# All first expert products ahead of the second ones, gates multiplied into an arena of ones, loops unrolled

## What is computed

```python
qh = (xt @ w_query).reshape(T, PEER_HEADS, PEER_KEY_DIM)
s1 = jnp.einsum('thd,nd->thn', qh[..., :half], sub_keys_1)
...
v1, i1 = lax.top_k(s1, PEER_TOPK)
...
top_s, top_j = lax.top_k(cand, PEER_TOPK)
...
u = expert_u[ec]
a = jax.nn.gelu(jnp.einsum('cd,ced->ce', xc, u).astype(jnp.float32), approximate=False)
return jnp.einsum('ce,ced->cd', (gc * a).astype(x.dtype), expert_v[ec])
```

## Time and profile before

| | us |
|---|---|
| time, median of 3 runs | 1217.26 |
| the three runs | 1221.36, 1217.26, 1208.93 |
| profiled execution, span from first to last instruction | 1207.1 |
| PE busy in it | 1091.6 (90%) |
| DVE busy in it | 685.5 (57%) |

### The profile page before, as it was taken

How to read it: one execution, slowest core, us unless ns; L and a number is a source line. 1 busy time by engine, 2 the same in 40 slices (tenths; PEclk the granted TensorE clock), 3 DMA queues, 4 the chain that set the end, 5 groups by cost and what they waited for, 6 DMA issues and landing times.

```text
span 1207.1 us, 19681 instructions
## 1 busy us (share of the span) xinstructions
PE 1091.6 (90%) x6268; PEld 942.4 (78%) x6268; DVE 685.5 (57%) x1678; ACT 480.8 (40%) x800; POOL 249.6 (21%) x332
## 2 busy tenths in 40 slices
PE   6997788979888677779999999999999999999994
PEld 2476667658788666668799999999999999999993
DVE  0112636037799669987755555555555555555554
ACT  0112424111333269963443444444434444444442
POOL 1000000000188858850011111111111111111110
PEclk9995556789988789999999999999999999999997
DMA  9830000050043200036545554555555545545541
GB/s 357 348 140 35 1 0 1 1 209 1 1 140 123 86 36 0 0 118 193 189 172 183 180 202 174 187 195 176 195 186 176 203 177 185 197 174 193 190 156 70
DMA packets 43516, 167.36 MB, mean 139 GB/s; under 512 B 4560, under 2 KB 5600, under 8 KB 41824
## 3 DMA queue, kind: packets, MB, share of 16 engines
q1 hardware_dynamic: 42944, 164.38, 38.0%
q0 software_dynamic: 544, 2.63, 0.5%
HBM read 165.94 MB, written 1.05 MB: 138 GB/s over the span
## 4 chain that ended last, share of the span: by engine, by line
PE 57%; issue 31%; POOL 5%; DVE 4%; ACT 2%; DVEq 1%; DMA 1%; POOLq 0%; ACTq 0%
PE ps L436 57%; POOL lo L403 4%; DVE slab L1296 2%; ACT arena L908 1%; DVE slab L1295 1%; DMA arena<-in_ln 1%; DVE arena L1285 0%; DVEq L1296 0%; DVE xs L1196 0%; DVE xs L1199 0%; DVE xs L1181 0%; PE ps L688 0%; DVE xs L1186 0%; POOL slab L417 0%; ACT L840 0%
## 5 line engine op out<-in xcount | busy, mean ns | idle before, releaser
L436 PE MATMUL ps<-x1hl,hi 128*128 128x256 f32 x2048 | 381.6, 287 | 22.2 <-POOL lo L403 21.4
L436 PEld LDWEIGHTS ps<-x1hl,hi 128*128 128x128 f32 x2048 | 333.2, 196 | 31.6 <-POOL lo L403 13.5
L436 PE MATMUL ps<-hi,ahl 128*128 128x512 f32 x1024 | 294.5, 393 | 3.4 <-DVE lo L1317 3.4
L436 PE MATMUL ps<-x1hl,lo 128*128 128x256 f32 x1024 | 293.5, 287 | 0.0
L1317 DVE TENSOR_TENSOR lo<-slab,hi 128x1024 fp32r<-128x1024 f32 x128 | 156.9, 1226 | 169.5 <-ACT hi L934 169.4
L934 ACT CAST hi<-slab 128x1024 fp32r<-128x1024 f32 x128 | 134.4, 1051 | 278.6 <-PE ps L436 278.6
L436 PEld LDWEIGHTS ps<-hi,ahl 128*128 128x128 f32 x1024 | 185.9, 189 | 37.5 <-issue 3.5
L436 PEld LDWEIGHTS ps<-x1hl,lo 128*128 128x128 f32 x1024 | 200.3, 196 | 0.0
L395 POOL TENSOR_TENSOR gel<-gel,arena 128x256 f32<-128x256 f32 x104 | 76.4, 735 | 577.6 <-ACT gel L940 577.6
L436 PE MATMUL ps<-lo,ahl 128*128 128x512 f32 x512 | 159.1, 392 | 0.0
L436 PE MATMUL ps<-arena 128*128 128x256 f32 (+6 forms) x608 | 153.6, 442 | 5.7 <-DVE arena L1065 2.0
(11 more groups left out here) (162 smaller groups left out, 762.4 us busy)
## 6 DMA issues: line engine op xcount, KB each, us to landing
slab<-in_uT SPq DMA_DIRECT2D x128, 512.0 KB, 4.1
slab<-in_pv SPq DMA_DIRECT2D x128, 512.0 KB, 3.5
arena<-in_w_tok SPq DMA_DIRECT2D x2, 2048.0 KB, 19.9
arena<-in_w_out SPq DMA_DIRECT2D x1, 4096.0 KB, 31.4
arena<-in_wqa SPq DMA_DIRECT2D x1, 4096.0 KB, 12.9
arena<-in_wqb SPq DMA_DIRECT2D x1, 4096.0 KB, 12.2
arena<-in_w_tok SPq DMA_DIRECT2D x4, 512.0 KB, 11.5
arena<-in_w_tok SPq DMA_DIRECT2D x1, 1792.0 KB, 19.3
```

What stands on the lines that cost most here:

```text
L436: return nc.tensor.matmul(o, lhsT, rhs, start=start, stop=stop, skip_group_check=True)
```

## The change

All 128 first products stand ahead of the 128 second ones. During routing DVE makes the rests itself, one by one between its own steps (`fill`, 35 of them), and the three passes over 6400 elements are cut in four pieces. The products of blocks 0 to 39 (`N0`) write their gelus into `arena`; POOL fills the rest of `arena` with 1.0 in two pieces. From block 40 on PE does one group of gates and one first product in turn; DVE multiplies every plate (128 blocks by 4 tokens) into `arena` (`gate_group`) and, one block at a time, the gelus of later blocks (`block_gate`). POOL no longer subtracts or multiplies; it makes two one-hots a group. The second products follow, with eight buffers for v and four for its high part. The transfer of the second norm's weights now starts after eight second blocks are split. Every loop is written out.

```diff
-NPRE = 24
+N0 = 40
+NROUTE = 35
+NTURN = 36
+UR, UH = 6, 3
+VR, VH = 8, 4
...
+            for c in range(NK):
+                if c >= UR:
+                    sp.wait_ge(pe_h, c - UR + 1)
+                sp.dma_start(u_raw(c), uT[c]).then_inc(u_in[c % UR], 16)
+            for c in range(NK):
+                if c == 0:
+                    sp.wait_ge(pe_g, GN)
...
+            pool.wait_ge(q_saved, 2 * PH)
+            nc.gpsimd.memset(arena[:, N0 * S:A_XT], 1.0).then_inc(ones_low, 1)
...
+            pool.wait_ge(rT_saved, T)
+            onehots(0)
+            onehots(1)
+            nc.gpsimd.memset(arena[:, A_XT:A_ALL], 1.0).then_inc(ones_high, 1)
+            for g in range(2, GN):
+                onehots(g)
+
+            pool.wait_ge(a_lo, KD)
             pool.dma_start(ln2_sb, ln2.partition_broadcast(P)).then_inc(l_ln2, 16)
...
+            for c in range(NK):
+                if c == NTURN:
+                    turn_routes()
+                if 0 <= c - N0 < GN:
+                    gates(c - N0)
+                expert_in(c)
...
+            for c in range(NK):
+                expert_out(c)
...
+            for c in range(NK):
+                gelu(c)
+                if c + UH < NK:
+                    u_split(c + UH)
+                if c + UH == NROUTE - 1:
+                    route_exp()
+                if c == NTURN - 1:
+                    save_routes()
+                    act.wait_ge(rT_saved, T)
+                    onehot(0)
+                if 0 <= c - (N0 - 1) < GN - 1:
+                    onehot(c - (N0 - 1) + 1)
...
+            def fill(n=1):
+                for _ in range(n):
+                    c = filled[0]
+                    dve.wait_ge(u_hi, c + 1)
+                    v.tensor_tensor(u_rest_of(c), u_raw(c), hi[:, c % UH, :].bitcast(F32), ALU.subtract).then_inc(u_lo, 1)
+                    filled[0] += 1
...
+            def gate_group(g, blocks):
+                dve.wait_ge(pe_g, g + 1)
+                if g == 0:
+                    dve.wait_ge(ones_low, 1)
+                    dve.wait_ge(ones_high, 1)
+                    dve.wait_ge(gelu_done, N0)
+                if blocks:
+                    dve.wait_ge(gated, blocks)
+                a = G[:, :, 4 * g:4 * g + 4]
+                v.tensor_tensor(a, ps[:, gate_bank(g), :].rearrange("p (q c) -> p c q", q=4), a, ALU.mult
                                 ).then_inc(pre_gated, 1)
...
+            while filled[0] < N0 - 1:
+                fill()
             dve.wait_ge(rT_saved, T)
-            onehots(0, True)
...
+            onehots(0)
+            fill()
+            for g in range(GN):
+                fill()
+                if g + 1 < GN:
+                    onehots(g + 1)
+                gate_group(g, max(0, g - 2))
+                if g >= 2:
+                    block_gate(N0 + g - 2, g + 1)
```

More of the change, by code:

```diff
@@ L337, in _ @@
             sp.wait_ge(pe_memp, 6)
[L339 to L375, removed]
+            for c in range(NK):
[5 more added lines that the diff above has]
+                    sp.wait_ge(pe_g, GN)
+                elif 4 <= c < VR:
+                    sp.wait_ge(pe_h, NK)
+                elif c >= VR:
+                    sp.wait_ge(pe_y, c - VR + 1)
+                sp.dma_start(raw[:, v_slot(c), :], pv[c]).then_inc(v_in[c % VR], 16)
             for t in range(T):
@@ L408, in onehots @@
[L408 to L418, removed]
@@ L667, in products @@
                     for m, (w, part) in enumerate(ws):
-                        last = mm(ps[:, b % 2, 0:S], w, x1hl[:, k, part, :], k == 0 and m == 0,
+                        last = mm(ps[:, c % 2, 0:S], w, x1hl[:, k, part, :], k == 0 and m == 0,
                                   k == KD - 1 and m == 2)
[L670 to L677, removed]
@@ L679, in _ @@
-            pe.wait_ge(x1_split, 2)
[L680 to L713, removed]
-            def expert_out(i, b, first, final):
-                pe.wait_ge(v_lo, i * RB + (b + 1))
-                pe.wait_ge(a_lo, i * RB + (b + 1))
+                last.then_inc(pe_h, 1)
@@ L720, in expert_out @@
[L720 removed]
+                    for m, (part, v) in enumerate(((0, vh), (0, vl), (1, vh))):
                         for half in range(2):
[L722 to L723 removed]
+                            last = mm(ps[:, 4 + 2 * t + half, :], ahl[:, c % 2, part, t * P:(t + 1) * P],
+                                      v[:, half * 512:(half + 1) * 512], c == 0 and m == 0, c == NK - 1 and m == 2)
@@ L952, in _, with gelu @@
-            with act.Fori(1, NM) as j:
-                for b in range(RB):
-                    u_split(j, b, False)
-                    gelu(j, b - 1, False)
-                    v_split(j + NP, b, False)
-            gelu(NM - 1, RB - 1, False)
+            def gelu(c):
+                act.wait_ge(pe_h, c + 1)
+                if c < N0:
+                    nc.scalar.activation(arena[:, c * S:(c + 1) * S], ps[:, c % 2, 0:S], ACT.Gelu).then_inc(gelu_done, 1)
+                else:
+                    if c >= N0 + 2:
+                        act.wait_ge(gated, c - N0 - 1)
+                    nc.scalar.activation(gel[:, c % 2, :], ps[:, c % 2, 0:S], ACT.Gelu).then_inc(gelu_done, 1)
@@ L958, in _ @@
+            for c in range(NK):
+                v_split(c)
             norm(1, range(T))
@@ L1356, in _ @@
+            for c in range(NK):
+                a_split(c)
+                v_rest(c)
             dve.wait_ge(l_ln2, 16)
```

366 lines of the change are left out of this document (155 added, 211 removed).

## The result

The changed kernel takes 1141.7 us (median of 4, 1140.7 to 1144.1), the kernel before 1214.4 in the same comparison (median of 4, 1208.9 to 1221.4): ratio 0.941, 95% interval 0.936 to 0.946. That is 73 us less; the prediction said 31 less, and its range ended at 1162.

A forecast was written before the change was run, and what follows sets the result against it. PE's own work bounds the kernel, with at most 69 us of pauses and 2.5 at the end to gain. Routing ready at 444.2 plus 731.9 gives span 1176.1, 31.0 under 1207.1; 1217.3 - 31 = 1186, range 1162 to 1225.

The forecast's parts named there:

- the ceiling: PE behind stage 1: 793 us of work takes 862, so pauses and slow clock can give 69 us at most.
- PE needs 1.15 + 2.87 = 4.02: 62 rounds of gates and product: PE sets the pace, DVE 0.2 behind; with small delays 4.15 a round, 257.3 us.
- R: The moment routing is ready: 332.7 + 68.0 + 40.3 + 1.6 + 1.6 = 444.2 us.
- The relief from POOL: Routing: without POOL's subtractions DVE's 80.7 us fall by 12.7 to 68.0; bounds 80.7 and 62.
- The fill of 1.0: POOL's memset behind routing takes 17.5 us; DVE's first plate waits for it and PE idles 7 us.
- The turn and the second products: After the last first product: 3 us of pause, 1.8 of slow clock, then 128 x 2.75 = 352 us.
- The end: After the second products: DVE starts 0.1 after PE instead of 2.5, norm weights long landed, then 15.5 us.
- From the span to the median: Whole kernel: the span falls 31.0 from 1207.1; taken off the median 1217.3, this gives 1186.
- Unrolling gives nothing: Whole kernel: loops cost nothing on PE now, so writing them out gives nothing by itself.
- DVE beside POOL's one-hots: Rival, gates: rests and gating each wait 0.61 for a one-hot; rounds 5.55, time 1273, or 1229 with half; chance 0.14.
- PE is fed by straight code: Against a rival: first products starved at 5.2 matmuls per us, 220 us more; chance 0.06 with anything else slower.
- The fill was not slow: Against a rival: POOL's memset takes 38 us, PE goes on 20.5 later, time 1207; chance 0.08.

The follow-up runs named there:

- the second execution: The changed kernel run again, nothing changed, on one chip beside the kernel with the second fill of 1.0 moved earlier: 1141.8 us, ratio to before 0.9435.

## Why the prediction was right and wrong

*What bounds.* PE does, as said, and the gain came from before the second products. But the ceiling, "793 us of work in 862, 69 us of pauses", was too low. With prices from start to start, PE's work is 128 x (2.86 + 2.72) + 64 x 0.88 = 771 us. Before, that left 91 us of pauses. After, PE takes from 332.5 to 1126.7, 794 us, with 23 left. The 68 between are the gain in the trace (62 at PE's end, and a first product that starts 5.6 later). So the gain of 73 lies above what the prediction held possible.

*The step that failed: "PE needs 1.15 + 2.87 = 4.02", and with it rounds of 4.15.* 1.15 is the length of a row. In the gates alone it is the delay until the result is there, which a wait needs; beside other matmuls the next one starts 0.82 behind, and a round is 3.77 - 2.86 = 0.91 longer than a first product alone. I had taken 0.07 off DVE's rows for just that reason and not looked at PE's. The rounds are 3.77, 62 x 0.38 = 23.6 us of the 33.9. Of the 0.38, 0.25 is the group's price (4.02 against 3.77) and 0.13 the small delays that I had added on top and that did not come. Doubling the gates measures the price as 0.88, and the rounds' bound is PE on both sides: 0.64 more on DVE costs 23 us, 0.2 less gives nothing. The mechanism, PE first and DVE 0.2 behind, was as forecast.

*Routing.* R was forecast at 444.2 and came at 440.6, although PE's first product began at 332.5 in this execution; with it at 326.8 (the second execution) R was 434.9, 9.3 early. That the first came within 3.6 is luck: its late start hid the difference. From the first tile's cast to the last step DVE takes 100.0 us. Of the 35 rests 32 lie there, 36.5 us; with the prediction's 3.2 for pieces and small steps, 60.3 is left for DVE's own work, where I had 68.0. The relief from POOL is 20 and not 12.7; the bound of 62 held nearly. With the rests on POOL the multiply pass alone loses 8 x 2.07 = 17 of that again.

*The fill of 1.0.* 13.76 us and not 17.5, 0.84 ns an element. PE did stand once behind the first groups, 4.7 us where I had 7. But the wait did not go through the plate, which found the ones ready: it went through the one-hots of the second group, which could not run beside the fill at all. I had no term for that, so the near size is luck.

*The turn and the second products.* PE's pause of 3 us was right; no slow clock followed it (1.00 from 765 to 790 us), so the 1.8 for that was too much. A second product takes 348.42 / 128 = 2.72 against the 2.75 of the earlier trace rows, 3.6 us in all. In the trace of before, too, second products that follow one another at the end take 2.73 (1184.47 to 1187.20), so the place beside first products may hold most of the difference; no run here tests it. The end was right: 0.1 us after PE, no wait for weights, then 15.5.

*From the span to the median.* I took 31 off the median of 1217.3. The execution profiled was 1208.93, the fastest of the four, and the one after stands 2.3 above its median. That adds 5.5 + 2.3, and the median before moved by 2.8: 33.9 + 10.6 = 44.5, the distance from 1186 to 1141.7.

*Unrolling gives nothing:* shown, in the kernel before. *The rivals:* DVE beside POOL's one-hots lost next to nothing; a rest takes 1.25 against 1.22. POOL does start when PE ends a group, beside the plate (564.04 and 563.98), as argued against that rival, but the traces show more than that: where POOL's one-hots lie across the whole rest, with three of them on POOL, it takes 1.27. The price of 0.61 for each meeting was wrong in itself. PE is fed by straight code at 257 matmuls in 30 us. The fill was not slow.

What stays open: the stages ahead of the first product end anywhere from 326 to 332 us in these executions, with or without the change. The traces show what goes with it, the stretch from 200 to 250 us in the first execution of the changed kernel and in its second (granted clock behind the counts):

```profile
200.00:250.00 50.00, 47.78 (x175) 34.01 (x175) 13.35 (x45) 13.71 (x33) 0.00 (x0) 0.73 0.00 0
200.00:250.00 50.00, 46.01 (x180) 30.43 (x177) 13.97 (x43) 12.57 (x27) 0.00 (x0) 0.86 0.00 0
```

Of the changed kernel and its variants, the six executions in which that number is 0.86 start their first product at 326.3 to 327.0; with 0.83 and 0.79 it is 328.4 and 329.8, and with 0.73 or 0.74, 330.4 to 332.5. So in the late ones PE stays longer at the lower of its two clock levels (1.2 and 2.4 GHz). What decides that is not shown, and I made no experiment on it.

## What to carry to other kernels

From these traces: price a matmul group by the distance from its start to the next one's start, in a stretch where PE has no wait; the length of a row is close to what a dependent engine waits, and is 0.2 to 0.3 us more for each group. A stage in which PE runs short groups at another engine's pace is worth moving beside long products, even when the two together leave both engines over 90% busy. An engine that only helps can cost more than it gives: here 35 subtractions on POOL stretched DVE's routing by more than the 36.5 us that 32 of them take DVE there.

## What was not expected of the hardware

POOL's fill of an SBUF tile stops DVE's one-hots (a tensor_scalar in fp32, SBUF to SBUF) until it ends: 10.62 us in the changed kernel, 4.82 in the one with the earlier fill. In that second one the rest, a tensor_tensor with two inputs in SBUF, runs at 1.23 beside the same fill. With POOL subtracting, DVE's multiply pass, a tensor_tensor, goes from 1.82 to 3.89.

The Trainium skill, page "SBUF — State Buffer", section "Who interferes with whom", bears on both. It says that a DVE instruction with two SBUF inputs contends with a GpSimd instruction that reads SBUF, not with one that only writes it. It also says that a tensor_scalar can enter a mode with both of the ports that DVE shares with GpSimd; whoever issues first then keeps them for its whole instruction, and the other is blocked. On the fill the traces agree with both, 10.62 against 1.22 beside one fill. On reads they agree in part: the multiply pass is slowed, the compare pass hardly (2.08), and a rest beside POOL's one-hots, which read SBUF, takes 1.27 for 1.22. The rule says who can meet, not what it costs; that is read from rows. I had used the first half of it and not asked it about the fill.
